# Owed work and a seed copy reordered between paired seven-product up blocks, weaker waits in the down blocks, an early square-root activation

## What is computed

```python
h2 = rmsnorm(x, norm_mlp)
return x + jnp.square(jax.nn.relu(h2 @ w_up)) @ w_down      # D_FF = 4096
```

## Time and profile before

| what | value |
|---|---|
| median of 3 runs | 2154.45 us (2154.25 to 2154.5) |
| the profiled execution | 2154.07 us |
| its span, first to last instruction | 2152.3 us |
| PE busy / DVE busy / ACT busy | 2113.6 / 1404.9 / 942.5 us |
| mean granted TensorE clock | 0.996 |
| read from HBM | 208.14 MB, 98 GB/s over the span |

### The profile page before, as it was taken

How to read it: one execution, slowest core, us unless ns; L and a number is a source line. 1 busy time by engine, 2 the same in 40 slices (tenths; PEclk the granted TensorE clock), 3 DMA queues, 4 the chain that set the end, 5 groups by cost and what they waited for, 6 DMA issues and landing times.

```text
span 2152.3 us, 27708 instructions
## 1 busy us (share of the span) xinstructions
PE 2113.6 (98%) x11086; PEld 1861.2 (86%) x11086; DVE 1404.9 (65%) x1956; ACT 942.5 (44%) x1351; POOL 1.4 (0%) x6
## 2 busy tenths in 40 slices
PE   9999999999999999999999999999999999999997
PEld 8878878878888888888899898888888888899896
DVE  8788785768665645655776676765435655776675
ACT  5776564645443322224452454443312234553452
POOL 0000000000000000000000000000000000000000
PEclk9999999999999999999999999999999999999998
DMA  5333212223222333333232333222333333232332
GB/s 181 111 105 108 88 60 79 79 80 102 79 93 93 98 98 104 102 99 97 88 111 86 118 110 107 87 79 91 105 100 106 88 109 107 89 108 89 118 108 79
DMA packets 59537, 212.03 MB, mean 99 GB/s; under 512 B 6737, under 2 KB 7121, under 8 KB 59281
## 3 DMA queue, kind: packets, MB, share of 16 engines
q1 hardware_dynamic: 59040, 208.83, 30.7%
q0 software_dynamic: 224, 1.31, 0.2%
q10 hardware_dynamic: 144, 0.12, 0.0%
HBM read 208.14 MB, written 2.10 MB: 98 GB/s over the span
## 4 chain that ended last, share of the span: by engine, by line
PE 78%; DVE 5%; ACT 3%; issue 1%; DVEq 0%; ACTq 0%
PE bank L750 21%; PE bank L752 20%; PE bank L751 20%; PE bank L793 2%; PE bank L797 2%; PE bank L795 2%; PE bank L745 2%; PE bank L746 2%; PE bank L747 2%; DVE w_lo L1667 1%; ACT w_hi L1154 1%; PE bank L987 1%; PE bank L979 1%; ACT arena L1471 0%; PE bank L1057 0%
## 5 line engine op out<-in xcount | busy, mean ns | idle before, releaser
L1667 DVE TENSOR_TENSOR w_lo<-w_raw,w_hi 128x1024 fp32r<-128x1024 f32 x423 | 507.8, 1214 | 548.4 <-ACT w_hi L1154 547.2
L1154 ACT ACTIVATE w_hi<-w_raw 128x1024 fp32r<-128x1024 f32 x423 | 437.1, 1046 | 721.6 <-PE bank L752 651.6
L750 PE MATMUL bank<-h_both,w_hi 128*128 128x512 f32 x1404 | 535.0, 381 | 2.2 <-DVE arena L1716 1.1
L751 PE MATMUL bank<-h_both,w_hi 128*128 128x512 f32 x1404 | 532.1, 379 | 0.0
L752 PE MATMUL bank<-h_both,w_lo 128*128 128x512 f32 x1404 | 532.1, 379 | 0.0
L750 PE MATMUL bank<-y_hi,w_hi 128*128 128x512 f32 x1048 | 399.8, 382 | 8.4 <-DVE y_lo L1721 3.4
L751 PE MATMUL bank<-y_lo,w_hi 128*128 128x512 f32 x1048 | 397.9, 380 | 0.0
L752 PE MATMUL bank<-y_hi,w_lo 128*128 128x512 f32 x1048 | 397.8, 380 | 0.0
L750 PEld LDWEIGHTS bank<-h_both,w_hi 128*128 128x128 f32 x1404 | 265.3, 189 | 42.5 <-issue 3.5
L751 PEld LDWEIGHTS bank<-h_both,w_hi 128*128 128x128 f32 x1404 | 265.4, 189 | 38.0 <-issue 1.0
L752 PEld LDWEIGHTS bank<-h_both,w_lo 128*128 128x128 f32 x1404 | 265.4, 189 | 37.6
(11 more groups left out here) (276 smaller groups left out, 2521.7 us busy)
## 6 DMA issues: line engine op xcount, KB each, us to landing
w_raw<-in_stream SPq DMA_DIRECT2D x389, 512.0 KB, 3.6
x<-in_x_t SPq DMA_DIRECT2D x8, 256.0 KB, 7.1
out_t<-x SPq DMA_DIRECT2D x8, 256.0 KB, 2.1
arena<-in_consts POOLq DMA_DIRECT2D x1, 1024.0 KB, 5.1
w_raw<-in_stream SPq DMA_DIRECT2D x2, 256.0 KB, 4.5
arena<-in_positions POOLq DMA_DIRECT2D x1, 256.0 KB, 5.9
vec_t<-in_vecs ACTq DMA_DIRECT2D x1, 112.5 KB, 3.3
ident<-in_consts SPq DMA_DIRECT2D x1, 64.0 KB, 6.8
```

Source lines behind the costliest of these rows:

```text
L750: pe.matmul(out, w_hi[:, slot, w], streamed(a_h), start=first, stop=False)
L751: pe.matmul(out, w_hi[:, slot, w], streamed(a_l), start=False, stop=False)
L1154: A.activation(w_hi[:, slot, w], w_raw[:, chunks.raw_slot[raw], w], ACT.Copy).then_inc(hi_ready, 1)
L1667: V.tensor_tensor(w_lo[:, slot, w], src[:, w], w_hi[:, slot, w].bitcast(F32), ALU.subtract).then_inc(lo_ready, 1)
```

## The change

It has four parts.

1. **ACT, in `seven`.** The relu of the sum bank now comes ahead of the high words of tiles 2 and 3. In a pair, what follows it is put on a list `owed` in four pieces: the high word of the tenth chunk, the high words of tiles 2 and 3, the squares, the high words of tiles 0 and 1. The second block pays them: two pieces behind its first seed copy, one behind the copy of `lent`, one behind the third copy and `ahead(5)`. `ahead(5)` itself moves, in both blocks, from in front of the copy behind product 3 to behind it.
2. **DVE, in `seven`.** `ahead(10)` stands in front of the low words of tiles 2 and 3; the two pairs of low words are owed too and paid in front of `ahead(4)` and behind `ahead(5)`. In the second block of a pair the order on DVE is the old one.
3. **PE, in `of_y`.** A scaled down block waits at each k for the count of its own tile, from a mark that each up block sets.
4. **ACT, in `squares`.** A square root of a 128 x 1 tile of constants is added behind the four squares of the last layer.

```diff
@@ PE @@
             def up(step):
+                T.mark["up", step.args["j"]] = T.value("a_lo")
...
                         pe.wait_ge(a_lo, T.mark["y", b, at] + (n - at + 1))
+                    elif step.args.get("scaled") and first:
+                        pe.wait_ge(a_lo, T.mark["up", k // 4] + k % 4 + 1)
                     elif first:
                         pe.wait_ge(a_lo, T.value("a_lo", k + 1 - n_k))
@@ ACT, seven @@
+            def pay(count=None):
+                for _ in range(len(owed) if count is None else min(count, len(owed))):
+                    owed.pop(0)()
...
                 products(1)
                 keep(sum_, first)
-                run_left_over()
+                pay(2)
                 ahead(4)
                 products(2)
                 keep(kept(T, 0), lent)
-                ahead(5)
+                pay(1)
                 products(3)
                 keep(last, sum_)
+                ahead(5)
+                pay(1)
                 ahead(6)
...
                 ahead(9)
-                for n in (2, 3):
-                    act.wait_ge(vec, T.value("vec", n + 1))
-                    hi(n, up_t[:, n, :], slot + n)
                 act.wait_ge(bank_ready, done)
                 positive(sum_, slice(SEQ // 2, SEQ)).then_inc(evacuated, 3)
-                ahead(10)
...
+                if step.args["paired"]:
+                    owed.extend((next_chunk, last_highs, first_squares, first_highs))
+                else:
+                    last_highs()
+                    next_chunk()
+                    first_squares()
+                    first_highs()
@@ ACT, squares @@
                     square(k, k)
+                A.activation(small[:, 79:80], eps_t[:, :], ACT.Sqrt)
@@ DVE, seven @@
+                pay(1)
                 ahead(4)
-                run_left_over()
-                for n in range(5, 9):
+                ahead(5)
+                pay(1)
+                for n in range(6, 9):
                     ahead(n)
...
-                low(2, 1)
-                low(3, 2)
-                ahead(10)
-                left_over.append(lambda: (low(0, 3), low(1, 4)))
-                if not step.args["paired"]:
-                    run_left_over()
+                if step.args["paired"]:
+                    ahead(10)
+                    owed.extend((last_lows, first_lows))
+                else:
+                    last_lows()
+                    ahead(10)
+                    first_lows()
```

More of the change, by code:

```diff
@@ L1148, in round_ahead, with round_raw @@
                 raw, made = raw_of(T, n)
+                round_raw(raw, made, slot, slice(0, used_columns(T, n)))
+            def round_raw(raw, made, slot, w):
                 if made:
@@ L1217, in seven, with last_highs, first_squares @@
                 ahead(9)
-                for n in (2, 3):
-                    act.wait_ge(vec, T.value("vec", n + 1))
-                    hi(n, up_t[:, n, :], slot + n)
                 act.wait_ge(bank_ready, done)
                 positive(sum_, slice(SEQ // 2, SEQ)).then_inc(evacuated, 3)
-                ahead(10)
-                outs = T.value("act_out")
-                def rest():
+                outs, made, next_slot_ = T.value("act_out"), T.value("vec"), (T.fixed["chunk"] + 10) % RING
+                def last_highs():
+                    for n in (2, 3):
+                        act.wait_ge(vec, made + n + 1)
+                        hi(n, up_t[:, n, :], slot + n)
+                def first_squares():
                     for n in range(2):
@@ L1232, in rest, with next_chunk @@
                         hi(n, up_t[:, n, :], slot + n)
-                left_over.append(rest)
-                if not step.args["paired"]:
-                    run_left_over()
+                raw, combined_at = raw_of(T, 10)
+                def next_chunk():
+                    round_raw(raw, combined_at, next_slot_, slice(0, CW))
+                if step.args["paired"]:
[5 more added lines that the diff above has]
+                    first_highs()
             def mix(step):
@@ L2365, in mix, with pay @@
                                     mixed[:, 0, n].bitcast(F32), ALU.subtract).then_inc(a_lo, 1)
-            left_over = []
-            def run_left_over():
-                while left_over:
-                    left_over.pop(0)()
+            owed = []
+            def pay(count=None):
+                for _ in range(len(owed) if count is None else min(count, len(owed))):
+                    owed.pop(0)()
             def seven(step):
@@ L2402, in seven, with last_lows, first_lows @@
                                            op0=ALU.max, op1=ALU.mult).then_inc(vec, 1)
[L2403 to L2408 removed]
+                def last_lows():
+                    low(2, 1)
+                    low(3, 2)
+                def first_lows():
+                    low(0, 3)
+                    low(1, 4)
+                if step.args["paired"]:
[5 more added lines that the diff above has]
+                    first_lows()
             def mixed_k(n, k):
```

9 lines of the change are left out of this document (2 added, 7 removed).

## The result

| | before | after |
|---|---|---|
| median | 2154.36 us (2153.53 to 2155.09, 6 runs) | 2137.83 us (2137.09 to 2138.02, 6 runs) |
| the profiled execution | 2154.07 us | 2137.09 us |
| its span | 2152.3 us | 2135.3 us |
| granted clock, mean | 0.996 | 0.996 |

The ratio is 0.9923, with a 95% interval of 0.991 to 0.9935: 16.5 us less, where 17.9 were forecast (2136.6). The range, 2135.0 to 2139.8, holds the median.

The account below looks back on a forecast made before the run. PE was taken as the bound, busy 2113.6 of 2152.3 us, so only its waits count. Terms 13.0 + 3.6 + 1.3 = 17.9 us, off 2154.45, gave 2136.6 us; range 2135.0 to 2139.8.

Parts of the forecast that it names:

- Six pairs, 13.0: Pairs of seven-product blocks: relu and seed copy first removes PE's wait at the second block's third product, 13.0 us in all.
- some 1.65 us are lost: First pair, behind PE's 1.97 us wait for the seed copy: time lost to the granted clock falling to 0.50.
- The margins: Second block of a pair: fourth, fifth and seventh products keep 2.1, 1.2 and 1.3 us to spare, so cost nothing.
- The third raw load: First block of a pair: moving the sixth chunk's rounding delays this load by 0 to 0.7 us; taken as 0.
- Quarter 0, 3.6: Down block of quarter 0: waiting by own tile removes PE's wait at the second k, 1.78 us in each of two layers.
- Square root, 1.3: End of the kernel: an early square root takes the 1.28 us table load off the path behind PE's sums.
- the second rival: Pairs: fifth or seventh product still waits 0.2 to 1.3 us, giving back 2.6 to 9.2 us; 2139.2 to 2145.8; chance 0.12.
- the first rival: Half-clock stretch comes back at a wait left at the end, so 1.65 us stay: 2138.2 us; chance 0.05.
- the fifth (load and drain): At the end, the square root's table costs load and drain, so 1.4 us more go: 2135.2 us; chance 0.02.
- a raw load of over 6 us beside the pair: Listed among the signs that would show the forecast wrong: a raw load this long beside a pair of seven-product blocks.
- the 0.02 for no change: Chance left for a measurement between the rivals on the faster side and the slower one, indistinguishable from no change.
- the third chain: Second block's seventh product needs the second kept copy, behind a rounding that waits for a raw load; 1.3 us to spare.

Follow-up runs that it names:

- the order alone: Kernel before with only the new order on ACT and DVE, down-block waits and square root as before: 2140.53 us, ratio 0.994.
- the sixth chunk put back: Changed kernel with the sixth chunk's rounding back in front of the copy behind product 3: 2136.56 us.
- the spare chunks left out: Changed kernel without the high and low words of the three empty chunks behind the last real one: 2135.39 us, ratio 0.9916 to the kernel before.
- the kept copy in front: Changed kernel without the empty chunks' words, second kept copy ahead of the eighth chunk's rounding in each seven-product block: 2143.17 us, ratio 0.9949.
- all paid at once: Changed kernel with ACT paying all four owed pieces at once behind the seed copy, DVE as changed: 2138.62 us, ratio 0.9926.

## Why the prediction was right, and where it was off

- **Six pairs, 13.0.** Measured 12.98, all pairs at 37.52, nothing waiting in them. The part of it that isn't the change's is the first pair's clock: "some 1.65 us are lost" held in the profiled execution and in the one with the new waits, but not in the one with the early root. As a gain over any execution the term is 11.4 to 13.0. The 3.0 us between PE's idle time (10.0) and this sum are that clock and a restart of 0.24 us behind each of six waits.
- **The margins.** Given as 2.1, 1.2 and 1.3 us to spare. The fourth product's low word ended at 1104.95 for a product due at 1107.08, 2.1. The fifth's was 1.3, and spare work confirmed it from both sides. The seventh's was 1.5 here; a landing of 5.6 us used it up in another run.
- **The third raw load.** Issued at 1091.34 (forecast about 1092.5; the program stood 1.1 us earlier), landed at 1094.96: 3.6 us, within the range given. It cost nothing.
- **Quarter 0, 3.6.** Measured 1.77 for each layer, 3.54; by the medians with this part alone 3.55. The 1.78 that was forecast holds.
- **Square root, 1.3.** This term was mis-sized: it gave 1.0. The step that failed is the reading that the table load's 1.28 us lie wholly between PE's sums and the root and would all go. Before, the load started 0.09 us behind the sums, and the root 1.39; with the table there, the root starts 0.41 us behind the sums. So 0.3 us of handing over from PE to ACT, read from these times, had run beside the load and came back when it went.
- **The rivals.** None came. A wait of the second rival's kind came only where a load was slow, work was added or the order was changed again: the 30 pairs in five profiles of the new order (the changed kernel's two, the order alone, the sixth chunk put back, the spare chunks left out) have none. For the first rival (half clock elsewhere), place alone doesn't decide: at one and the same place the clock fell in some executions and not in others, and no run shows what decides. For the fifth (load and drain), no drain beside the load shows in the changed kernel: the instruction before it ends at 2103.81, the load runs from 2103.83 to 2105.11, and the early root starts at 2105.12. The sign "a raw load of over 6 us beside the pair" was too wide: loads of 6.8, 6.6 and 6.2 us lie beside pairs of 37.52 us in the order alone, with the sixth chunk put back and without the spare chunks. Only the load that the kept copy stands behind has so small a margin.
- **The chances.** The forecast and its five rivals already add up to 1.00, so the 0.02 for no change stands beyond them.
- **The sum.** 13.0 + 3.5 + 1.0 = 17.5 us for the two profiled executions; 17.0 were measured. The rest is the first row of the table above: the start of the program, which the change doesn't touch, took 0.64 us more. There PE's clock was at its lower level for some 3 us in the profile after, and not before (the stretch 12 to 13 us, before, then after):

```profile
12.00:13.00 1.00, 1.00 (x7) 0.78 (x6) 1.00 (x3) 1.00 (x3) 0.00 (x0) 1.00 1.00 395
```

```profile
12.00:13.00 1.00, 1.00 (x4) 0.73 (x3) 1.00 (x3) 1.00 (x3) 0.00 (x0) 0.50 1.03 404
```

By medians the gain was 16.5 and 16.2 us in the two measurements, 0.5 and 0.8 less than between the profiles, and the first median lies 1.2 us above the forecast. Only profiled executions have a trace, so where these lie stays open. The traces do show that what the change doesn't touch differs by more than that. Ten profiles have the new waits and the same program up to the first pair, and reach it between 1079.2 and 1081.5 us, the four latest with the granted clock low for some 7 us from about 162.5 on. Six have the changed kernel's program behind the last pair, and take 57.3 to 59.6 us there. That the terms' sum fits two profiles to 0.5 us is in part luck; that each pair and each quarter 0 fits is not. The three parts alone gave 13.8, 3.55 and about 1.0 us, 18.3 in all, and the interval of the first is wide enough (9.7 to 16.2 us) to hold the difference.

## What to carry to other kernels

An instruction whose inputs have long been ready and whose reader is the bound engine belongs in front of work that waits for a slower neighbour; then follow each thing that was moved behind it to its next reader, and keep 1 to 2 us there if it stands behind a load: the load of the third chain landed up to 2 us later than usual, 5.6 us for 3.6. When a line is run by several blocks, follow it in each of them: an order that is right for the second block can undo the first. And price a removed operation by the end of what released it to the start of what follows, not by its own length.

## What the hardware showed that was not expected

- The same idle time of PE of 1.97 us, at the same place of the same order, was followed by the 1.2 GHz level in two profiled executions and not in a third. An idle time of 2.31 to 2.32 us brought it in one pair of three, 3.41 in three of three, 1.60 to 1.63 in none of the fifteen of the three kernels with the old order in the pairs.
- Behind a wait of PE a pair grew by 0.23 to 0.24 us more than the idle time that the profile lists where PE waited for ACT (0.54 for 0.31, 0.81 for 0.57, 1.08 for 0.85, 1.84 for 1.60), and by 0.27 where it waited for DVE (0.99 for 0.72), with the clock at its upper level throughout. The first matmul behind the wait starts some 0.16 us later than idle time and usual distance make it, the second one 0.07 to 0.10.
- Short stalls are missing from the list of PE's waits: with the kept copy in front five pairs grew by 1.13 us for a listed 0.53, and 0.33 us of that stand at the fourth product, which the list doesn't name.
- The landing of a 512 KB weight load is 3.6 to 3.7 us at the median of the whole program, but 4.5 for those issued during the pairs, and the longest of these took 5.9 to 7.2 us, by profile. The one load that the third chain stands behind took 3.5 to 3.9 us in 30 of 36 pairs (the changed kernel twice, the order alone, the sixth chunk put back, all paid at once, the spare chunks left out) and 4.1 to 5.6 in six, all of them second or fourth pairs.
- The granted clock is low for some microseconds at the start in some executions (11 to 15 us), 0.50 to 0.67 of full speed in the changed kernel's first profile and 1.00 in the kernel before's; all later times then stand about half a microsecond later.
